# A Trainium2 decoder-layer kernel: the down projection's output tiles in pairs by block products, and attention scores in two passes on 128 rows

## What is computed

```python
h = rmsnorm(x, g_ffn1);  x = x + 0.5 * swiglu(h, w1_a, w3_a, w2_a)
h = rmsnorm(x, g_mix);   proj = h @ w_in
q_sb, k_sb, v_sb, q_dl, k_dl, v_dl, gate_pre = jnp.split(proj, split_points, axis=-1)
gates = jax.nn.sigmoid(gate_pre + b_gate);  g_sb, g_dl = split(gates)
y_sb = merge_heads(stick_breaking_attention(q_sb, k_sb, v_sb)) @ w_sb_out        # 8 heads
y_dl = merge_heads(dilated_window_attention(rope(q_dl), rope(k_dl), v_dl)) @ w_dil_out
x = x + (g_sb * y_sb + g_dl * y_dl) @ w_o
h = rmsnorm(x, g_ffn2);  x = x + 0.5 * swiglu(h, w1_b, w3_b, w2_b)
return rmsnorm(x, g_final)
# swiglu(h, w1, w3, w2) = (silu(h @ w1) * (h @ w3)) @ w2
# stick breaking: A[t,s] = beta[t,s] * prod_{s<j<t} (1 - beta[t,j]), s < t, beta = sigmoid(q.k / 8)
# dilated: 12 query heads in 3 groups (window, stride) = (128,1), (512,4), (2048,16) over 4 key heads,
#          a softmax a group, the groups' outputs mixed by their softmax denominators
```

## Time and profile before

| | |
|---|---|
| median of 3 runs | 1125.85 us (1125.63 to 1126.07) |
| the profiled execution | 1127.22 us as a whole, a span of 1125.3 us |
| PE busy | 1101.4 us, 98% of the span |
| DVE busy | 770.2 us, 68% |
| ACT busy | 543.7 us, 48% |
| GpSimd (POOL) busy | 2.7 us |
| granted TensorE clock, mean | 0.997 of full speed |

### The profile page before, as it was taken

One profiled execution on the slowest core, in us unless ns is written; L12 is line 12 of the kernel. 1 busy time (PEld: TensorE's weight loads), 2 busy tenths in 40 slices (PEclk: granted clock), 3 DMA queues, 4 the chain that ended last, 5 costly groups with the idle time before them and its releaser, 6 DMA issues.

```text
span 1125.3 us, 15594 instructions
## 1 busy us (share of the span) xinstructions
PE 1101.4 (98%) x6033; PEld 943.5 (84%) x6033; DVE 770.2 (68%) x1090; ACT 543.7 (48%) x870; POOL 2.7 (0%) x6
## 2 busy tenths in 40 slices
PE   8999999999999999999999999999999999999996
PEld 6888899988998788877777778788898899889985
DVE  7876378745868778678765556667774578637864
ACT  6554155523644456567755543425552355415642
POOL 0000000000000000000000000000000000000000
PEclk9999999999999999999999999999999999999999
DMA  8323233332324212111112113422233323333222
GB/s 295 96 75 113 75 113 113 113 94 94 93 73 131 79 39 75 56 38 53 51 57 75 52 57 96 142 94 94 90 104 106 95 94 113 94 94 113 82 68 75
DMA packets 34295, 103.18 MB, mean 92 GB/s; under 512 B 4144, under 2 KB 7472, under 8 KB 34224
## 3 DMA queue, kind: packets, MB, share of 16 engines
q1 hardware_dynamic: 34224, 102.21, 28.9%
HBM read 100.10 MB, written 2.10 MB: 91 GB/s over the span
## 4 chain that ended last, share of the span: by engine, by line
PE 85%; DVE 6%; ACT 4%; issue 3%; SPq 1%; DMA 1%; POOL 0%; POOLq 0%; DVEq 0%; ACTq 0%
PE acc_pair L1208 24%; PE acc_pair L1209 24%; PE acc_pair L1210 24%; PE pair_bank L1208 2%; PE pair_bank L1210 2%; PE pair_bank L1209 2%; DVE w_lo L785 1%; PE bank L1208 1%; PE bank L1210 1%; PE bank L1209 1%; ACT rope L646 1%; ACT w_hi L487 1%; DMA w_raw<-in_w13a 1%; PE bank L1216 1%; PE bank L1218 1%
## 5 line engine op out<-in xcount | busy, mean ns | idle before, releaser
L1208 PE MATMUL acc_pair<-xg_hi,w_hi 128*128 128x512 f32 (+1 forms) x693 | 265.5, 383 | 1.5 <-DVE w_lo L1016 1.5
L1209 PE MATMUL acc_pair<-xg_lo,w_hi 128*128 128x512 f32 (+1 forms) x693 | 259.8, 375 | 0.0
L1210 PE MATMUL acc_pair<-xg_hi,w_lo 128*128 128x512 f32 (+1 forms) x693 | 259.1, 374 | 0.0
L487 ACT ACTIVATE w_hi<-w_raw 128x1024 fp32r<-128x1024 f32 (+3 forms) x159 | 154.3, 976 | 147.9 <-PE acc_pair L1210 147.3
L785 DVE TENSOR_TENSOR w_lo<-w_raw,w_hi 128x1024 fp32r<-128x1024 f32 (+3 forms) x159 | 178.6, 1126 | 42.3 <-ACT w_hi L487 41.3
L1210 PEld LDWEIGHTS acc_pair<-xg_hi,w_lo 128*128 128x128 f32 x693 | 130.5, 188 | 24.6
L1208 PEld LDWEIGHTS acc_pair<-xg_hi,w_hi 128*128 128x128 f32 x693 | 130.8, 189 | 23.1 <-issue 2.8
L1209 PEld LDWEIGHTS acc_pair<-xg_lo,w_hi 128*128 128x128 f32 x693 | 131.0, 189 | 19.9 <-issue 0.7
L1210 PE MATMUL acc_pair<-hid_hi,w_lo 128*128 128x512 f32 x352 | 138.8, 394 | 0.0
L1209 PE MATMUL acc_pair<-hid_lo,w_hi 128*128 128x512 f32 x352 | 138.2, 393 | 0.0
L1208 PE MATMUL acc_pair<-hid_hi,w_hi 128*128 128x512 f32 x352 | 136.9, 389 | 0.0
(11 more groups left out here) (220 smaller groups left out, 2059.7 us busy)
## 6 DMA issues: line engine op xcount, KB each, us to landing
w_raw<-in_w13b SPq DMA_DIRECT2D x44, 512.0 KB, 3.6
w_raw<-in_w13a SPq DMA_DIRECT2D x40, 512.0 KB, 3.8
w_raw<-in_wmix SPq DMA_DIRECT2D x22, 512.0 KB, 3.5
w_raw<-in_w2a SPq DMA_DIRECT2D x16, 512.0 KB, 3.6
w_raw<-in_w2b SPq DMA_DIRECT2D x16, 512.0 KB, 3.5
...
```

What stands on the lines that cost most here:

```text
L487: act.activation(w_hi[:, s, 0:width], w_raw[:, s, 0:width], ACT.Copy).then_inc(whi_done, 1)
L1208: pe.matmul(o, w_h, r_h, start=first, stop=False, skip_group_check=check)
L1209: pe.matmul(o, w_h, r_l, start=False, stop=False, skip_group_check=check)
L1210: return pe.matmul(o, w_l, r_h, start=False, stop=last, skip_group_check=check)
```

## The change

**Down projection.** The output tiles of the down projection are taken in pairs, 11 an FFN: 4 in each chunk of 8 hidden tiles, 3 in the last (its tiles 6 and 7 stay plain). The two halves of k are `HQ = 2` hidden tiles each (`HID_PAIRS`; w2's rows are reordered to match), the other tiles are plain. A chunk therefore needs sums of hidden tiles, `th_hi` and `th_lo`, made for two pairs of tiles as they are finished. DVE now takes both outputs of the pair before in one piece (`take_outputs`) ahead of the split of the next weights, and ACT does a pair's squares behind its third seed.

**Attention.** An operand of the scores has 128 rows per head: `sq2` and `dq2` hold a head's high part in its 64 rows and its low part in the other 64; `sk2`, `dk2` hold the key's high part in both, the second copy made by a DMA from SP (`twin_done`, L559); `sk_lo`, `dk_lo` hold its low part and zeros (memsets on POOL). One matmul `sk2` by `sq2` gives high by high plus high by low, a second with `sk_lo` the rest. ACT and DVE split these tiles in two halves of 64 rows. k is computed ahead of q. The high parts `spA_hi` go from DVE to ACT. `cos`, `sin` and `mask_dl` are loaded behind the weights of unit MIX+8, and DVE waits for them and scales the tables ahead of head 0's scores.

```diff
+HQ = 2
+HID_PAIRS = {(0, 0): ((0, 1), (4, 5)), (1, 0): ((2, 3), (4, 5))}
-MIX_ORDER = ([("q", 0, 0), ("k", 0, 0), ("v", 0, 0), ("q", 1, 0), ("k", 1, 0), ("v", 1, 0),
+MIX_ORDER = ([("k", 0, 0), ("q", 0, 0), ("v", 0, 0), ("k", 1, 0), ("q", 1, 0), ("v", 1, 0),
...
@@ SP
+                if u == MIX + 8:
+                    sp.wait_ge(unit_done, MIX)
+                    sp.dma_start(cos[:], A["cos"]).then_inc(late_loaded, 16)
...
+                if u - 7 in KEYS:
+                    sp.wait_ge(op_hi_done, split_parts(u - 7 - MIX + 1))
+                    for head in (0, 1):
+                        key = stacked(u - 7, head).bitcast(F32)
+                        sp.dma_start(key[head_rows(head + 1), :], key[head_rows(head), :]).then_inc(twin_done, 16)
@@ ACT
+            def fast_pair(u, prev, nxt, n_next):
...
                 split_hi(u + 2, 0, unit_width(u + 2))
                 act.wait_ge(p6_done, g + 1)
                 act.activation(r3, r2, ACT.Copy, scale=-1.0).then_inc(seed2, 1)
...
                 act.wait_ge(p7_done, g + 1)
                 act.activation(r4, r2, ACT.Copy).then_inc(seed3, 1)
...
+                if prev is not None and before is None and down_unit(prev)[1] == len(CHUNKS) - 1:
+                    if down_unit(prev)[2] == 0:
+                        act.preload_act_table_set("sqrt_and_others")
+                    squares(prev, n_next)
...
+                if before is not None:
+                    hidden_sums_hi(prev)
...
+                        for head in (0, 1):
+                            rows = head_rows(head)
+                            act.activation(stacked(w, head)[rows, :], src[rows, :], ACT.Copy).then_inc(op_hi_done, 1)
...
+                        act.activation(spA_hi[:, cols], ebuf[:, cols], ACT.Copy).then_inc(a_hi_done, 1)
@@ DVE
+            def hidden_sums(u):
...
+                dve.tensor_tensor(hsum[:, 0], b12, b11, ALU.subtract).then_inc(hsum_done, 1)
...
+            def take_outputs(u, n_next):
+                _, c, m = down_unit(u)
+                add_fifth(u)
+                for k in (0, 1):
+                    s, before = update_x(u + k, m + k, 0.5)
+                    if c == len(CHUNKS) - 1:
+                        if n_next < 3:
+                            dve.wait_ge(acc_read[s], before + 1)
+                            prep(m + k, n_next)
+                        add_square(m + k, n_next)
+
+            def fast_pair(u, prev, nxt, n_next):
...
+                elif prev is not None:
+                    take_outputs(prev, n_next)
+                split_lo(u + 2, 0, unit_width(u + 2))
...
+                if kind == "scores" and w == 0:
+                    dve.wait_ge(late_loaded, 16 * N_LATE)
...
-                        dve.tensor_copy(spA_hi[:, cols], ebuf[:, cols]).then_inc(a_hi_done, 1)
@@ PE
                 pe.wait_ge(seed2, g + 1)
-                quarter_products(r2, sh[:, 0], sl[:, 0], t_hi[:, 2], t_lo[:, 2]).then_inc(p7_done, 1)
+                quarter_products(r2, sh[:, 0], sl[:, 0], sums(u, 2)).then_inc(p7_done, 1)
...
-                            product(o, sk_hi[rows, hp % 2, ks], sk_lo[rows, hp % 2, ks],
-                                    sq_hi[rows, hp % 2, P * i:SEQ], sq_lo[rows, hp % 2, P * i:SEQ],
-                                    n == 0, False, True)
+                            pe.matmul(o, sk2[:, hp % 2, a, ks], sq2[:, hp % 2, a, P * i:SEQ], start=n == 0,
+                                      stop=False, skip_group_check=True)
+                            pe.matmul(o, sk_lo[:, hp % 2, a, ks], sq2[:, hp % 2, a, P * i:SEQ], start=False,
+                                      stop=False, skip_group_check=True)
```

598 lines of the change are left out of this document (365 added, 233 removed).

## The result

The changed kernel took **1140.35 us**, the median of 4 runs (1138.74 to 1142.42). Against runs of the kernel before it is slower by 1.2%: the ratio is 1.0122, with a 95% interval of 1.0100 to 1.0143. The forecast was 1128.9 us with a range up to 1134. The direction was right and the size was not: 14.5 us were lost where 3.0 were forecast.

What follows compares the result with a forecast made beforehand. TensorE, busy 1101.4 of 1125.3 us, was taken to bound the kernel. FFNs +11.0 us and attention -8.0 made +3.0 on the 1125.85 us median: 1128.9 us, range 1118.5 to 1134.

Steps and rivals of the forecast that it cites:

- The clock: TensorE's clock falls to half behind two new waits in the FFNs' last chunks: +3.4 us, bounds 0 and 3.4.
- the two new waits of the last chunks: Second pair of each FFN's last chunk: TensorE idles 3.2 us for split weights; +6.6 us with first intervals.
- the two starts' waits: FFN starts: hidden sums lengthen the first's w_lo wait from 0.8 to 3.0 us, the second's ACT wait by 2.0.
- The sum of the rest: All terms but the clock's: FFNs +11.0 us including 3.4 for the clock, attention -8.0.
- Waits in the FFNs: Last chunks' second pairs wait about 3.2 us on w_lo; starts' waits grow to 3.0 and by 2 us.
- The second seed: Down pairs: third product waits for ACT's negated copy, 0.36 us in 16 pairs (+5.8), 0.13 in 6 (+0.8).
- the products: Down projection: 42 matmuls of 256 columns replace 24 of 512, gaining 0.49 us a pair, -10.8 us over 22.
- The seventh unit: First FFN, after the last chunk's second pair: the split for this unit ends late, +0.5 us.
- Attention: Two passes replace three: at most -24.2 us; -8.0 after late heads (-1.5), blocks 0 to 3 (+2.6), later blocks (-9.4), end (+0.3).
- the key copies: Attention: copies of key high parts have about 4 us to the scores and cost nothing.
- the halves: Attention tiles split in two 64-row halves: about 0.6 us more per engine and tile; 0.85 us in the blocks' loop.
- the loop: Dilated blocks 0 to 3: ACT and VectorE's 8.66 us from exp to exp grows 0.85 us, 3 times: +2.6 us.

Runs made afterwards that it cites:

- stalls: The kernel before with eleven waits for GpSimd memsets added in its down projections, nothing else changed: 1175.42 us, ratio 1.0422.
- seed_ahead: The changed kernel with ACT's second seed of a down pair put ahead of the rounding of the next unit's weights: 1135.63 us, ratio 1.0075.
- twin_early: Changed attention with the down projection of before, key copies issued one load of weights earlier on SP: 1126.86 us, ratio 1.0000 to the kernel before.

## Why the prediction was wrong, step by step

**The clock: the step that failed.** "I count a fall for each, +3.4 us; the bounds are 0 and 3.4." The step took the two new waits of the last chunks alone, took 1.7 us a fall from the one row of before, and let the 2.4 us of the earlier trace rows without a fall speak against more. Measured: 13.6 us net in the profiled execution. Three things were wrong in it. It priced a wait at one stretch of 3.41 us, where 3 of the 7 are 6.8. It gave the two starts' waits (3.0 and 3.3 us, which the same text forecast) no fall, though they are as long as the two that got one. And it gave the attention's waits none. With the sum's other terms as they were, 13.6 for 3.4 makes +13.2 us, 1139.1. The sentence that the bounds are 0 and 3.4 is why the range failed too. In `stalls` four added waits of 2.66 to 3.09 us had half clock. The Trainium skill ("TensorE: Matmul & The Clock Gate", Part 1: The HAM clock gate) lets the clock fall after an idle stretch past a limit, which the FFNs' waits do not reach; by that rule they would cost nothing beyond themselves. The rows of `stalls` disagree, and they decide.

**The sum of the rest is close by luck.** Without the clock (TensorE's busy time in the stretches, halved) the FFNs (up to the first scores, and from w_o to the last transposes) lost 5.3 us where 7.6 stood (11.0 less 3.4), and the attention gained 5.4 where 8.0 stood. The two misses cancel: together about 0, where the forecast had -0.4. These are estimates too, since where ACT and VectorE set the pace, as in the first dilated blocks, half clock need not cost TensorE anything.

**Waits in the FFNs: right, to 0.1 us.** Forecast 3.2 on w_lo in the second pair of each last chunk, measured 3.14 and 3.10; "3.0 instead of 0.8" at the start, measured 3.06 for the earlier trace rows; "2 us longer" at the second FFN's first fast pair, measured 3.33 for 1.32, as in the earlier trace rows. They came from walking along ACT's and VectorE's programs with durations of single operations.

**The second seed and the products: right mechanism, some 2 us too dear.** A pair and its third product (timeline of PE):

```profile
113.49 0.28 PE L1395 MATMUL acc_pair<-th_hi,s_hi 128*128 128x256 f32 x1
115.13 0.39 PE L1395 MATMUL acc_pair<-th_hi,s_hi 128*128 128x256 f32 x1
115.35 0.28 PE L1396 MATMUL acc_pair<-th_lo,s_hi 128*128 128x256 f32 x1
124.24 0.28 PE L1395 MATMUL acc_pair<-th_hi,s_hi 128*128 128x256 f32 x1
```

The third product starts 1.64 us after the first (forecast 1.70), the first interval is 0.22, and the pair takes 10.75 us, where 10.87 followed from the sum (11.0 - 0.49 + 0.36) and 10.8 to 10.9 was written. `seed_ahead`'s 10.45 shows the term: 0.30 us a pair, not 0.36. Over 16 pairs the 0.12 between 10.87 and 10.75 are 1.9 us, most of what the FFNs were forecast too dear.

**The seventh unit** waited 0.26 us in the first FFN, not 0.5.

**Attention: -8.0 forecast, measured 334.10 for 334.91 us from the first scores to w_o, -0.8.** Half clock cost up to 6.3 us in it and 1.7 before, so -0.8 - 4.6 = -5.4 is to be compared with -8.0. Most of what is missing was lost in the heads. Up to the first dilated block the changed kernel falls 4.15 us further behind, 2.9 of it clock: 1.3 us lost where 1.5 were to be left. From there to the sixteenth block it gains 4.7 us, or 6.4 without the clock, where 6.8 were forecast. Behind the sixth block's scores the term is exact: 82.12 us from there to the sixteenth's before, 74.33 after, 0.78 a block for 0.79. Before head 7's suffix TensorE waited 4.12 us, where waits of 1 to 3 were forecast. And two terms failed. "I cost them at nothing" for the key copies: TensorE waited 2.09 us for one. It left out that a copy stands behind a load in SP's order (with the copy ahead, in `twin_early`, that wait is gone), and that it takes its own time: the eight copies of `sk` took a median of 4.2 us from issue to landing. And the halves: a tile of 128 rows in two of 64 costs each engine its whole again,

```profile
550.40 1.28 ACT L801 ACTIVATE dk<-roped 64x512 fp32r<-64x512 f32 x2
```

```profile
551.78 1.41 DVE L1267 TENSOR_TENSOR dk_lo<-roped,dk 64x512 fp32r<-64x512 f32 x2 [2.51 <-ACT dk L801]
```

(timelines of ACT and VectorE), so 0.65 and 0.7 us more in a row, some 1.4 where 0.85 stood. The exponentials of blocks 1 to 4 before (two of the four; the others are in the earlier trace rows) and after,

```profile
535.38 0.94 ACT L724 ACTIVATE prob<-prob,stats 128x768 f32<-128x768 f32 x1 [0.46 <-DVE stats L1141]
561.36 0.95 ACT L724 ACTIVATE prob<-prob,stats 128x768 f32<-128x768 f32 x1 [0.34 <-DVE stats L1141]
```

```profile
546.88 0.94 ACT L848 ACTIVATE prob<-prob,stats 128x768 f32<-128x768 f32 x1 [0.47 <-DVE stats L1328]
557.57 0.94 ACT L848 ACTIVATE prob<-prob,stats 128x768 f32<-128x768 f32 x1 [0.34 <-DVE stats L1328]
567.41 0.94 ACT L848 ACTIVATE prob<-prob,stats 128x768 f32<-128x768 f32 x1 [0.34 <-DVE stats L1328]
576.73 0.94 ACT L848 ACTIVATE prob<-prob,stats 128x768 f32<-128x768 f32 x1 [0.34 <-DVE stats L1328]
```

were 9.49, 8.66 and 7.83 us apart and are 10.69, 9.84 and 9.32: each is 1.2 to 1.5 us longer, together +3.9 for +2.6. The forecast had read one of the three intervals and took its 8.66 us for all; their mean happens to be the same. On TensorE the loop shows one block later than forecast: from the fifth block's scores to the sixth's it takes 9.65 us, where it took 8.26 before and 7.5 was forecast.
